# Two transformer blocks in one kernel: the order of work in the state-space stage and in the inner norms

## The reference, cut to what matters

```python
def first_block(x, ...):
    h = rms_norm(x, norm_mix_w)
    z, xbc, dt_raw, q, k, v, f_raw = split(h @ w_in)
    y_ssd = ssd_mixer(xbc, z, dt_raw, ...)      # state space, 16 heads, chunks of 128
    y_fox = fox_mixer(q, k, v, f_raw, ...)      # attention, 16 heads
    x = x + concatenate([y_ssd, y_fox]) @ w_out
    hf = rms_norm(x, norm_ffn_w)
    return x + conv_gated_mlp(hf, w_up, conv_w, conv_b, w_down)

def second_block(x, p, ...):
    z = rms_norm_2(x, mix_norm_g) @ w_in
    ...                                          # retention, sliding window attention
    merged = sigmoid(gate_r) * y_r + sigmoid(gate_s) * y_s
    x = x + merged @ w_out
    x = x + hierarchical_moe(rms_norm_2(x, ffn_norm_g), ...)   # 32 experts, top 2
    ple = rms_norm_2(p @ w_ple, ple_norm_g)
    return x + sigmoid(rms_norm_2(x, ple_gate_norm_g) @ w_ple_gate) * ple

# in ssd_mixer, per chunk c and head e
scores = cb[:, :, :, None] * decay               # decay = exp of differences of a running sum
y_diag = einsum(scores, xdt)
y_off = einsum(cm, states_in) * exp(a_cs)        # from the state before the chunk
y = y_diag + y_off + d_skip * x6
```

## Time and profile before

| what | value |
|---|---|
| median of 3 runs | 1588.07 us (1587.91 to 1588.78) |
| the profiled execution | 1588.81 us |
| its span | 1586.9 us |
| PE busy | 1528.1 us, 96% of the span |
| DVE, ACT, POOL busy | 805.2, 616.1 and 140.4 us |
| chain that ended last | PE 89%, DVE 6%, ACT 3%, DMA 1%, issue 1% |
| mean granted TensorE clock | 0.988 |

### The profile page before, as it was taken

One profiled execution on the slowest core, in us unless ns is written; L12 is line 12 of the kernel. 1 busy time (PEld: TensorE's weight loads), 2 busy tenths in 40 slices (PEclk: granted clock), 3 DMA queues, 4 the chain that ended last, 5 costly groups with the idle time before them and its releaser, 6 DMA issues.

```text
span 1586.9 us, 21123 instructions
## 1 busy us (share of the span) xinstructions
PE 1528.1 (96%) x7508; PEld 1110.8 (70%) x7508; DVE 805.2 (51%) x1486; ACT 616.1 (39%) x1176; POOL 140.4 (9%) x160
## 2 busy tenths in 40 slices
PE   7999999999999999999999999999997999999959
PEld 6777788845887888888887888877786333333337
DVE  4867764677335666656235346764556222222156
ACT  5656543467324455554224322555236100000033
POOL 1014300010000000000000001100001122222110
PEclk9999999999999999999999999999999999999979
DMA  6333233210232333333333321322254999999541
GB/s 207 114 99 94 87 110 96 86 61 28 86 94 86 94 98 96 96 99 93 100 95 98 95 85 54 120 67 80 80 176 157 408 411 409 408 388 382 201 178 54
DMA packets 93570, 232.96 MB, mean 147 GB/s; under 512 B 15664, under 2 KB 16176, under 8 KB 89264
## 3 DMA queue, kind: packets, MB, share of 16 engines
q1 hardware_dynamic: 80032, 209.75, 38.2%
q0 software_dynamic: 13168, 21.87, 4.1%
q10 hardware_dynamic: 288, 0.23, 0.0%
HBM read 282.05 MB, written 16.84 MB: 188 GB/s over the span
## 4 chain that ended last, share of the span: by engine, by line
PE 89%; DVE 6%; ACT 3%; DMA 1%; issue 1%; SPq 0%; POOL 0%; ACTq 0%; DVEq 0%; POOLq 0%
PE ps L350 21%; PE ps L351 21%; PE ps L352 21%; PE ps L1038 11%; PE ps L1057 5%; PE ps L1017 2%; DVE acc L2102 1%; PE ps L459 1%; ACT Pb L1991 1%; DVE lo L345 1%; PE ps L1767 1%; PE ps L1625 1%; PE ps L1755 1%; PE ps L1741 1%; DVE Pb L2344 1%
## 5 line engine op out<-in xcount | busy, mean ns | idle before, releaser
L345 DVE TENSOR_TENSOR lo<-raw,hi 128x512 fp32r<-128x512 f32 x288 | 198.4, 710 | 294.5 <-ACT hi L335 294.3
L335 ACT ACTIVATE hi<-raw 128x512 fp32r<-128x512 f32 x288 | 176.6, 632 | 387.5 <-PE ps L352 387.1
L350 PE MATMUL ps<-HTh,lo 128*128 128x512 f32 x688 | 269.9, 392 | 5.7 <-DVE HTl L423 3.6
L352 PE MATMUL ps<-HTh,hi 128*128 128x512 f32 x688 | 267.9, 389 | 0.0
L351 PE MATMUL ps<-HTl,hi 128*128 128x512 f32 x688 | 267.8, 389 | 0.0
L350 PEld LDWEIGHTS ps<-HTh,lo 128*128 128x128 f32 x688 | 129.1, 188 | 35.9 <-issue 3.6
L352 PEld LDWEIGHTS ps<-HTh,hi 128*128 128x128 f32 x688 | 129.2, 188 | 26.9
L351 PEld LDWEIGHTS ps<-HTl,hi 128*128 128x128 f32 x688 | 129.2, 188 | 26.1
L350 PE MATMUL ps<-hi,HTl 128*128 128x512 f32 (+1 forms) x352 | 138.4, 393 | 0.5 <-ACT zs L1861 0.4
L352 PE MATMUL ps<-hi,HTh 128*128 128x512 f32 (+1 forms) x352 | 134.8, 383 | 0.0
L351 PE MATMUL ps<-lo,HTh 128*128 128x512 f32 (+1 forms) x352 | 134.6, 382 | 0.0
(11 more groups left out here) (389 smaller groups left out, 2505.3 us busy)
## 6 DMA issues: line engine op xcount, KB each, us to landing
raw<-in_wstream SPq DMA_DIRECT2D x384, 256.0 KB, 2.6
slot<-in_wexp SPq DMA_DIRECT2D x64, 1024.0 KB, 18.6
slot<-in_wexp SPq DMA_DIRECT2D x16, 2048.0 KB, 18.1
cum<-cum_d POOLq DMA_DIRECT2D x16, 256.0 KB, 3.9
fcb<-fc_d POOLq DMA_DIRECT2D x16, 256.0 KB, 3.5
YG<-ye_d SPq DMA_DIRECT2D x3, 1024.0 KB, 9.3
X<-in_x SPq DMA_DIRECT2D x4, 512.0 KB, 5.7
xg_d<-xn POOLq DMA_DIRECT2D x4, 512.0 KB, 4.2
```

Of the source, the lines that this page charges most:

```text
L335: act.activation(hi[:, i % RING, :], raw[:, i % RING, :], ACT.Copy).then_inc(hi_ready, 1)
L345: dve.tensor_tensor(lo[:, i % RING, :], raw[:, i % RING, :], hi[:, i % RING, :].bitcast(F32), ALU.subtract).then_inc(lo_ready, 1)
L350: pe.matmul(o, al, bh, start=start, stop=False)
L352: return pe.matmul(o, ah, bh, start=False, stop=stop)
```

## The change

Six edits, in the order of the program.

1. ACT's Exp for `tok[:, 3]` moves from ahead of the first `tokens_x` to behind the four `silu_z(0, t)`.
2. DVE's `from_state(0, 1)` moves behind `values(0)` and `score(5)`.
3. The inner norms get their own helpers. The sum of squares of the last token tile is made in two halves: columns 0 to 511 (which were summed long before) right behind tile 0's squares, columns 512 to 1023 after the last addition. DVE turns the first half into a mean ahead of time (`small[:, 60]`), and joins the two in one small instruction.
4. DVE scales the last tile in two halves of 512 columns; chunks 0 to 3 may be transposed after the first.
5. PE transposes tiles 0 to 2 without waiting for the last addition, except for the chunk whose bank that addition reads (`last`); that one follows.
6. The four sigmoids `gs1` are no longer mixed with splits, and PE waits for them bank by bank, as `free` of `so0`.

```diff
+        def act_add_norm(act, n, xnb, wname):
+            def square(t, c0, c1, at_):
+                return act.activation(xnb[:, t, c0:c1], X[:, t, c0:c1], ACT.Square, accum_out=small[:, at_:at_ + 1])
+
+            for t in range(T - 1):
+                act.wait_ge(x_res, XRES(n, t))
+                square(t, 0, D, t).then_inc(n_ss, 1)
+                if t == 0:
+                    square(T - 1, 0, 512, 59)
+            act.wait_ge(x_res, XRES(n, T - 1))
+            square(T - 1, 512, D, T - 1).then_inc(n_ss, 1)
...
-        def dve_add_norm(dve, n, xnb, wname, name, s_):
+        def dve_add_norm(dve, ch, n, xnb, wname, name, s_):
...
-                norm_mean(dve, n, t)
-            norm_scale(dve, n, T - 1, xnb)
+                if t < T - 1:
+                    norm_mean(dve, n, t)
+                if t == 1:
+
+                    ch.mark(dve.tensor_scalar(small[:, 60:61], small[:, 59:60], 1.0 / D, EPS, ALU.mult, ALU.add))
+            dve.wait_ge(n_ss, T * n + T)
+            ch.wait()
+            dve.scalar_tensor_tensor(small[:, 3 + T:4 + T], small[:, T - 1:T], 1.0 / D, small[:, 60:61], ALU.mult, ALU.add
+                                     ).then_inc(n_ms, 1)
+            dve.wait_ge(n_rstd, T * n + T)
+            for hf in range(2):
+                cc = slice(512 * hf, 512 * hf + 512)
+                dve.tensor_scalar(xnb[:, T - 1, cc], X[:, T - 1, cc], small[:, 7 + T:8 + T], None, ALU.mult).then_inc(n_xn, 1)
             norm_rest(dve, n, wname)
...
+        def pe_add_norm(pe, n, xnb, last):
+
+            def turn(t, c):
+                return pe.transpose(ps[:, c, t * P:(t + 1) * P], xnb[:, t, c * P:(c + 1) * P], ident[:, :])
+
+            pe.wait_ge(x_res, 8 * n - 1)
+            for t in range(T - 1):
+                pe.wait_ge(n_xn, XN(n) + t + 1)
+                for c in range(DC):
+                    if c != last:
+                        turn(t, c)
+            pe.wait_ge(x_res, 8 * n)
+            for t in range(T - 1):
+                turn(t, last)
+            for c in range(DC):
+                if c % 4 == 0:
+                    pe.wait_ge(n_xn, XN(n) + T + c // 4)
+                turn(T - 1, c).then_inc(n_tr, 1)
...
                 if b:
                     pe.wait_ge(m_s, 4)
-                else:
-                    pe.wait_ge(b2c, 40)
-                pe_features(pe, U[f"so{b}"], 4, 1, ysh, ysl)
+                pe_features(pe, U[f"so{b}"], 4, 1, ysh, ysl, free=None if b else (b2c, 36))
...
             w.upto(U["ro0"] + 8)
-            w.beside(U["ro1"] + 4, [copy(gs[1][:, j, :], ps[:, 4 + j, :], "gs1", ACT.Sigmoid) for j in range(4)])
+            for j in range(4):
+                copy(gs[1][:, j, :], ps[:, 4 + j, :], "gs1", ACT.Sigmoid)()
+            w.upto(U["ro1"] + 4)
...
             silu_x(11)
-            act.wait_ge(tok_ready, 2)
-            act.activation(tok[:, 3, :, :], tok[:, 1, :, :], ACT.Exp).then_inc(etok, 1)
...
             for t in range(T):
                 silu_z(0, t)()
+            act.wait_ge(tok_ready, 2)
+            act.activation(tok[:, 3, :, :], tok[:, 1, :, :], ACT.Exp).then_inc(etok, 1)
...
             score(4)
-            from_state(0, 1)
             values(0)
             score(5)
+            from_state(0, 1)
             w.upto(U["q0"] + 2)
```

More of the change, by code:

```diff
@@ L409, in act_norm @@
                                scale=col(wname, c)).then_inc(n_hi, 1)
+        def act_add_norm(act, n, xnb, wname):
[9 more added lines that the diff above has]
+            for c in range(DC):
+                act.wait_ge(n_tr, DC * n + c + 1)
+                act.activation(HTh[:, c, :], ps[:, c, :], ACT.Identity, scale=col(wname, c)).then_inc(n_hi, 1)
         def norm_mean(dve, n, t):
@@ L413, in norm_mean, with XN @@
             dve.tensor_scalar(small[:, 4 + t:5 + t], small[:, t:t + 1], 1.0 / D, EPS, ALU.mult, ALU.add).then_inc(n_ms, 1)
+        def XN(n):
+            return T * n + max(n - 1, 0)
         def norm_scale(dve, n, t, xnb):
@@ L479, in PE_B2 @@
             U = FIRST
-            pe_norm(pe, 2, xn2, [(x_res, 16)])
+            pe_add_norm(pe, 2, xn2, 3)
             pe_features(pe, U["rq"], 8, 0, HTh, HTl, ready=(ht_lo, 16), free=(ht_lo, 16))
@@ L652, in ACT_B2 @@
             U = FIRST
-            act_norm(act, 2, xn2, "nmix2")
+            act_add_norm(act, 2, xn2, "nmix2")
             def copy(dst, src, name, func=ACT.Copy, after=()):
@@ L738, in DVE_B2 @@
             U = FIRST
-            dve_add_norm(dve, 2, xn2, "nmix2", "down1", 0)
+            dve_add_norm(dve, ch, 2, xn2, "nmix2", "down1", 0)
             w.upto(U["rq"] + 8)
@@ L972, in PE_MOE @@
             U = FIRST
-            pe_norm(pe, 3, xn3, [(x_res, 24)])
+            pe_add_norm(pe, 3, xn3, 7)
             for u in range(2):
@@ L1083, in turn @@
             def turn(t):
-                pe.wait_ge(n_xn, 4 * T + t + 1)
+                pe.wait_ge(n_xn, XN(4) + t + 1)
                 if t >= 2:
@@ L1130, in ACT_MOE @@
             w.upto(FIRST["ple0"] + 2)
-            act_norm(act, 3, xn3, "nffn2")
+            act_add_norm(act, 3, xn3, "nffn2")
             w.upto(MOE_AT)
@@ L1222, in DVE_MOE @@
             U = FIRST
-            dve_add_norm(dve, 3, xn3, "nffn2", "mo1", 1)
+            dve_add_norm(dve, ch, 3, xn3, "nffn2", "mo1", 1)
             w.upto(U["ple1"] + 1)
@@ L1432, in POOL_MOE @@
             for t in range(T):
-                pool.wait_ge(n_xn, 3 * T + t + 1)
+                pool.wait_ge(n_xn, XN(3) + t + 1 + t // (T - 1))
                 pool.dma_start(xg_d[t * P:(t + 1) * P, :], xn3[:, t, :]).then_inc(xg_st, 16)
@@ L1791, in _ @@
             pe_tokens_last(pe, U["out1"] + 12, 1, MIXh1, MIXl1, 4)
-            pe_norm(pe, 1, xnF, [(x_res, 8)])
+            pe_add_norm(pe, 1, xnF, 7)
             u = U["up0"]
@@ L2027, in _ @@
             w.upto(U["up0"] + 4)
-            act_norm(act, 1, xnF, "nffn")
+            act_add_norm(act, 1, xnF, "nffn")
             w.upto(U["up0"] + 8)
@@ L2400, in _ @@
             w.upto(U["up0"] + 4)
-            dve_add_norm(dve, 1, xnF, "nffn", "out1", 1)
+            dve_add_norm(dve, ch, 1, xnF, "nffn", "out1", 1)
             w.upto(U["up0"] + 8)
```

## The result

| | before | changed |
|---|---|---|
| median of 5 runs, us (lowest to highest) | 1588.57 (1587.91 to 1589.30) | 1580.36 (1579.38 to 1581.09) |
| profiled execution, us | 1588.81 | 1580.17 |
| its span, us | 1586.9 | 1578.4 |

The ratio is 0.995, 95% interval 0.994 to 0.9961: 8.2 us faster, where 9.8 were forecast. The predicted 1578.3 is 2.1 under the median. The changed kernel, timed again with the last experiments, gave 1578.94 (ratio 0.9941, 0.9927 to 0.9955), so a median of five moves by over 1 us between two timings of the same code.

A forecast was written before the change was run, and what follows sets the result against it. PE's own work, busy 96% of the span, was taken as the bound; gains 1.5 + 1.8 + 3.0 + 2.2 + 1.3 = 9.8 us off 1588.81 gave 1579.0, median 1578.3 us, range 1576.2 to 1583.3.

The forecast's parts named there:

- Edit 1, forecast 1.5: First copy `xs`: without load and Exp ahead, PE's wait shrinks from 2.1 us to about 0.6; gain 1.5 us.
- The score multiply's cover: First score multiply: comes about 1.3 us earlier instead of 1.5, with 1.9 us of cover before its products.
- Edit 2, forecast 1.8: Head 4: values(0) starts 1.78 us earlier, leaving 0.76 of PE's 2.54 us wait; gain 1.8 us.
- I keep that for the range: Head 5: its score multiply may take 1.56 us instead of 0.69, so PE would wait up to 0.6 us.
- the sum was 9.2: Head 5: by the shared-interface rule GpSimd holds the moved score multiply, making the total gain 9.2 us, not 9.8.
- The clock, forecast 3.0: Behind head 4's wait: with less idle time the granted clock does not fall; gain 3.0 us, bounds 2.7 to 3.3.
- the rival that it falls all the same: Behind head 4: the clock still falls, so the 3.0 us are missing and time is 1581.3 us; chance 0.15.
- Edits 3 to 5, forecast 2.2: Three inner norms: the chain after the last addition is 0.72 us shorter at each; gain 2.2 us.
- edit 6, forecast 1.3: Second gate's sigmoid copies: PE's 1.26 us wait for the last of four goes; gain 1.3 us.
- The rival of the stretch at 324: Low clock at 324 us and elsewhere shortens, gaining 1.5 (1576.8 us), chance 0.06; last sentence: could equally cost 1.5.
- DVE and GpSimd take back the whole gain: Around head 4: a longer split or late score loses the 4.8 us won there, clock included; 1583.1 us, chance 0.10.
- three or more held instructions that cost it: Heads 5 to 9: GpSimd holds DVE, 3.87 us per instruction; slower from the third, four give 1593.8 us; chance 0.02.

The follow-up runs named there:

- The same order with PE busy in the wait: Changed kernel with values(0) again behind from_state, plus 36 zero-adding matmuls on PE before head 4: 1581.69 us, ratio 0.9952.
- the filler at the last gate: Changed kernel plus 125 unread identity transposes on PE before the last gate's first turn, behind the wait for the experts' output: 1589.39 us.

## Why the prediction was nearly right

**Edit 1, forecast 1.5: right.** The wait went from 2.1 to 0.49, and undone it costs 1.6. The score multiply's cover held.

**Edit 2, forecast 1.8: right, less 0.8.** The wait at head 4 shrank by 2.54 - 0.74 = 1.8, as worked out. The term that was mis-sized is head 5 waiting for its held score multiply, at nothing in the sum by "I keep that for the range". The estimate was 1.56 us and a wait of up to 0.6; it took 1.96 and the wait was 0.83. It belonged in the sum. The rule of the Trainium skill, GPSIMD Engine Reference, Specifications, on the shared interfaces, by which the sum was 9.2, was the better guide: both inputs of the held multiply lie in SBUF, while values(0), which reads PSUM, took 1.27 us for two beside GpSimd's 1.05. The same holds for score 4, 1.53 before and after: the prediction's rows show it by its length alone (the longest of 16 is 1.56), and without it the wait of 0.74 goes.

**The clock, forecast 3.0: right, with a doubt that was too small.** Undoing the order costs 3.8 in the heads, of which the waits are 1.0, so the fall is 2.8, near the lower bound of 2.7. That the first profile had no fall in the heads at all was in part luck: of eight, three had one. The same order with PE busy in the wait wins 1.4 of it back, even with a fall elsewhere. So the rival that it falls all the same, given 0.15, came in those three, at half its price: a loss of 1.5, not of 3.0.

**Edits 3 to 5, forecast 2.2: right** (2.2 by the runs with edits undone), **and edit 6, forecast 1.3** (1.6). The order of the norms' chain came as forecast: the earlier 24 transposes end 0.36 before the last tile's start, with 0.25 foreseen. What the other 0.3 of the gate is, the waits don't show.

**What was missing.** Forecast and spans differ by 9.8 - 8.5 = 1.3: 0.8 less at head 5, 0.1 more on the way to the router (3.6 for 2.2 and 1.3), 1.7 lost at the experts, 0.9 won at the end, and 0.2 at the start, which is of no edit. The experts and the end are where the low clock lasted longer or shorter, and a second profile of the same code gave 303.8 and 71.7 there in place of 305.7 and 70.3; so neither belongs to the change.

**The rival of the stretch at 324** was half right: it went away in the first profile, and nothing was won. Before, PE waited once for `fst`:

```profile
PE ps L1741 <- DVE fst L2344: 1.3, 1, 1.3
```

The products that ran at half clock from there on let the second `fst` come in time; at full clock PE is early and waits for it, 2.5 in two. Attention takes 202.2 with either. So the 1.5 that I took as a price of the low clock there was covered by a wait: removing that fall wins nothing. In two other profiles (the changed kernel again, edit 5 undone) both waits are there and the clock falls too, but some 8 us further on in the program, behind the waits, where nothing covers it: 203.6, the loss that this rival's last sentence allowed for. The other rivals (DVE and GpSimd take back the whole gain; three or more held instructions that cost it) didn't come: three score multiplies were long in place of two, and only the new one, head 5's, was a loss against the kernel before.

## What to carry to other kernels

When a VectorE instruction with both inputs in SBUF is moved to a moment at which GpSimd multiplies, price it as held (here 1.53 to 1.96 us in place of 0.68), in the sum and not in the range alone; moving GpSimd's work away may only choose the next one to be held. A wait of TensorE can cost more than its length, through the granted clock behind it, but put a chance on that, and look at what comes next: a wait that the slow stretch covered takes its place. Where medians of five differ by 1 us from one timing to the next, cut the traces at the same instructions and compare stretch by stretch; and before filling an idle stretch, see which wait in the code it belongs to.

## What was unexpected in the hardware

The same code had different stretches of low clock in different profiles: none or 1.7 us of low-clock loss behind heads 4 and 5, none or 1.7 in attention, 3.4 or 5.1 at the experts' start, about 8.5 or 10.2 at the last gate. A wait of 2.1 us at the first copy brought a fall in one profile (edit 1 undone) and none in the kernel before. It is not the chip alone: the changed kernel again and the filler at the last gate, on one chip and with the same code up to there, differ in attention, 203.6 against 202.2. The forecast had these as fixed. This agrees with what the Trainium skill, TensorE: Matmul & The Clock Gate, What's actually happening, says of the two states, that the monitor runs free of the kernel. In the prediction it was given a chance of 0.06 as a gain and none of its own as a loss. Zero-adding products of 64 rows and 128 columns (2.19 us for 36) in place of the wait were enough to keep the clock at 1.00 behind head 4, in the one profile that has them.
